# Second layer: down product of the feed-forward and the last layer norm in one stage, by passes over token tiles

## What is computed

```python
    x = layer_norm(DN_ALPHA * x + mix, ln1_w, ln1_b)
    ffn = (jax.nn.silu(x @ ffn_w_gate) * (x @ ffn_w_up)) @ ffn_w_down
    return layer_norm(DN_ALPHA * x + ffn, ln2_w, ln2_b)
```

## Time and profile before

| What | Value |
|---|---|
| Median of 3 runs | 4682.42 us (4680.55 to 4683.03) |
| The profiled execution, own time | 4683.53 us |
| Its span in the profile | 4681.7 us |
| Mean granted TensorE clock | 0.894 of full |
| TensorE, VectorE, ScalarE busy | 80%, 53%, 32% of the span |

### The profile page before, as it was taken

The page is one execution under the profiler, slowest core; times in us unless marked ns, Lnnn a source line. Parts: engine busy times, 40 slices in busy tenths (PEclk is TensorE's granted clock), DMA queues, the critical chain, the costliest instruction groups (busy, mean ns, idle before and its releaser), DMA issues. The chain is left out here.

```text
span 4681.7 us, 62399 instructions
## 1 busy us (share of the span) xinstructions
PE 3759.1 (80%) x25544; PEld 3078.1 (66%) x25544; DVE 2488.5 (53%) x2686; ACT 1494.1 (32%) x1777; POOL 90.8 (2%) x57
## 2 busy tenths in 40 slices
PE   6999948887399999189995545437998788999994
PEld 5888847776377777178883234217996667888783
DVE  5773328944388889354412879664555542111235
ACT  3222114533177777221121232342332221111223
POOL 0000000000100000100000010000000000000002
PEclk8999979998599999589997677669999899999997
DMA  6422226423599999642222131352110432111113
GB/s 244 170 104 87 85 71 204 142 69 143 202 397 399 398 398 358 237 146 103 99 72 80 38 122 65 107 132 72 43 54 9 157 113 63 45 50 45 45 64 144
DMA packets 355375, 652.91 MB, mean 139 GB/s; under 512 B 53896, under 2 KB 149912, under 8 KB 352954
## 3 DMA queue, kind: packets, MB, share of 16 engines
q1 hardware_dynamic: 317482, 524.34, 32.5%
q10 hardware_dynamic: 26864, 83.37, 4.5%
q0 software_dynamic: 10784, 41.70, 2.2%
HBM read 489.23 MB, written 171.65 MB: 141 GB/s over the span
## 5 line engine op out<-in xcount | busy, mean ns | idle before, releaser
L155 PE MATMUL fu_ps<-x3T_hi,fu_w_lo 128*128 128x512 f32 x704 | 275.2, 391 | 9.5 <-DVE fu_w_lo L3055 9.5
L155 PE MATMUL g_ps<-x2T_hi,g_w_lo 128*128 128x512 f32 x704 | 275.1, 391 | 9.1 <-DVE g_w_lo L338 9.1
L156 PE MATMUL fu_ps<-x3T_lo,fu_w_hi 128*128 128x512 f32 x704 | 275.0, 391 | 0.0
L156 PE MATMUL g_ps<-x2T_lo,g_w_hi 128*128 128x512 f32 x704 | 274.8, 390 | 0.0
L157 PE MATMUL g_ps<-x2T_hi,g_w_hi 128*128 128x512 f32 x704 | 274.8, 390 | 0.0
L157 PE MATMUL fu_ps<-x3T_hi,fu_w_hi 128*128 128x512 f32 x704 | 274.8, 390 | 0.0
L382 DVE COPY g_st<-g_ps 128x512 f32<-128x512 f32 x40 | 27.7, 692 | 323.2 <-PE g_ps L157 323.2
L1497 DVE TENSOR_TENSOR moe_wg_lo<-moe_wg,moe_wg_hi 128x2048 fp32r<-128x2048 f32 x68 | 155.6, 2292 | 69.7 <-ACT moe_wg_hi L1451 69.7
L370 DVE SCALAR_TENSOR_TENSOR g_st<-g_pad,g_par,g_st 128x1024 f32<-128x1024 f32 x140 | 179.8, 1285 | 10.8 <-issue 0.4
L155 PE MATMUL g_ps<-h1T_hi,g_w_lo 128*128 128x512 f32 x448 | 175.6, 392 | 7.2 <-DVE g_w_lo L338 7.2
L156 PE MATMUL g_ps<-h1T_lo,g_w_hi 128*128 128x512 f32 x448 | 175.4, 392 | 0.0
(11 more groups left out here) (608 smaller groups left out, 9967.1 us busy)
## 6 DMA issues: line engine op xcount, KB each, us to landing
moe_wg<-in_exp_w_gate SPq DMA_DIRECT2D x68, 1024.0 KB
moe_wu<-in_exp_w_up SPq DMA_DIRECT2D x68, 1024.0 KB
moe_wd<-in_exp_w_down SPq DMA_DIRECT2D x66, 1024.0 KB
g_w<-in_w_in SPq DMA_DIRECT2D x96, 512.0 KB, 4.0
s_conv<-g_st ACTq DMA_DIRECT2D x14, 2048.0 KB, 6.9
s_xs<-g_zero POOLq DMA_DIRECT2D x1, 24064.0 KB
s_ys<-moe_y ACTq DMA_DIRECT2D x47, 512.0 KB, 6.3
moe_x<-s_xs SPq DMA_DIRECT2D x34, 512.0 KB
```

What stands on the lines that cost most here:

```text
L155: pe.matmul(out, l[1], r[0], start=(k == 0), stop=False)
L156: pe.matmul(out, l[0], r[1], start=False, stop=False)
```

## The change

`gemm_deep` for the down product and the `residual_norm` behind it are replaced by one stage, `deep_norm` (tiles also named `fd_`). The product is now made in three passes over token tiles, (0, 1, 2), (3, 4, 5) and (6, 7). A pass runs over k = 0 to 21; a unit n is one k of one pass, 66 units in all. In a unit the tiles of the pass are multiplied by all 1024 output columns, as two matmul columns of 512, into an accumulator of two PSUM banks per tile; four accumulators are used in turn. For each unit 128x1024 weights are loaded (512 KB) and split, and of `hid` only the pass's tokens (384, in the last pass 256 columns) are split. There are three buffers of each; the split halves lie in the memory of `xT`, which is free by then.

The x3 tiles are loaded to `r` (five buffers), at units 3 to 7 and, once the tile before in the buffer is stored, at k = 13 to 15 of the second pass. The norm of a pass's tiles is made in `r` in place while the next pass is multiplied: residual straight from PSUM behind k = 1, sums behind k = 2, centring and squares behind k = 3, variance behind k = 4, roots behind k = 5, the scaling of one tile each behind k = 6, 7 and 8, stores behind k = 10, 11 and 12. The last pass's tiles are normed after the product. The multiplication by the norm weight is on VectorE. `fo` is gone. The parts of `deep_norm` for `router`, `factor` and `sum_out` are not used in this call.

```diff
+def deep_norm(nc, name, aT, w_src, x, w, out, passes, alpha=1.0, bias=None, eps=EPS, factor=None, sum_out=None, room=None,
+              router=None, n_r=NT):
...
+    KT, layer, ND = aT.shape[1], bias is not None, D // P
...
+    NR, NB, NU = 3, 3, NP * KT
+    n_acc = 2 if router else 4
+    with Stage(nc, name) as s:
+        w_raw, r, sq = s.sb("w_raw", [P, NR, D]), s.sb("r", [P, n_r, D]), s.sb("sq", [P, D])
+        wr = s.sb("wr", [P, D])
+        br = s.sb("br", [P, D]) if layer else None
...
+        if room:
+            (w_hi, a_hi), (w_lo, a_lo) = ((h[:, 0:NB], h[:, NB:2 * NB, 0:TP * P]) for h in room)
...
+        acc = s.ps("acc", [P, n_acc, D])
...
+        def unit(n):
+            return n // KT, n % KT
+
+        def side(n):
+
+            g = passes[n // KT]
+            return slice(g[0] * P, g[0] * P + len(g) * P), len(g) * P
...
+            def load(t):
+                if t < NT:
+                    if t >= n_r:
+                        sp.wait_ge(stored[t % n_r], past(16 * (t // n_r)))
+                    sp.dma_start(r[:, t % n_r], x[t * P:t * P + P, :]).then_inc(x_in[t % n_r], 16)
...
+            def store(t):
+                sp.wait_ge(normed, past(t + 1))
+                sp.dma_start(out[t * P:t * P + P, :], r[:, t % n_r]).then_inc(stored[t % n_r], 16)
+
+            for n in range(NU):
+                p, k = unit(n)
+                if n >= NR:
+                    sp.wait_ge(w_low, past(n - NR + 1))
+                sp.dma_start(w_raw[:, n % NR], w_src[k * P:k * P + P, :]).then_inc(w_in[n % NR], 16)
+                if n == 2:
+                    for t, src in ((wr, w),) + (((br, bias),) if layer else ()):
+                        sp.dma_start(t[:, :], src.partition_broadcast(P)).then_inc(c_in, 16)
+                if 3 <= n < 3 + n_r:
+                    load(n - 3)
+                for i, t in enumerate(passes[p - 1] if p else ()):
+                    if k == 5 + i:
+                        store_sum(t)
+                    if k == 10 + i:
+                        store(t)
+                    if k == 13 + i and t + n_r >= n_r:
+                        load(t + n_r)
...
+            for t in passes[-1]:
+                store(t)
+            for b in range(n_r):
+                sp.wait_ge(stored[b], past(16 * len(range(b, NT, n_r))))
...
+            for n in range(NU):
+                p, k = unit(n)
+                pe.wait_ge(w_low, past(n + 1))
+                pe.wait_ge(a_low, past(n + 1))
+                for i, t in enumerate(passes[p]):
+                    if k == 0 and t >= n_acc:
+                        pe.wait_ge(added, past(t - n_acc + 1))
+                    for c in range(2):
+                        mm = products3(pe, acc[:, t % n_acc, c * 512:c * 512 + 512],
+                                       [h[:, n % NB, i * P:i * P + P] for h in (a_hi, a_lo)],
+                                       [h[:, n % NB, c * 512:c * 512 + 512] for h in (w_hi, w_lo)], k, KT)
+                    if k == KT - 1:
+                        mm.then_inc(done, 1)
+                if k < KT - 1:
+                    mm.then_inc(used, 1)
...
+        def free(eng, n):
+
+            if n >= NB:
+                p, k = unit(n - NB)
+                if k == KT - 1:
+                    eng.wait_ge(done, past(passes[p][-1] + 1))
+                else:
+                    eng.wait_ge(used, past(n - NB + 1 - p))
...
+        @block.scalar
+        def _(act):
+            def split(n):
+                p, k = unit(n)
+                o, m = side(n)
+                free(act, n)
+                act.wait_ge(w_in[n % NR], past(16 * (n // NR + 1)))
+                act.activation(w_hi[:, n % NB], w_raw[:, n % NR], ACT.Copy).then_inc(w_high, 1)
+                f = {} if factor is None else dict(scale=fac[:, k:k + 1])
+                act.activation(a_hi[:, n % NB, 0:m], aT[:, k, o], ACT.Copy, **f).then_inc(a_high, 1)
...
+            def total(g):
+                for t in g:
+                    act.wait_ge(added, past(t + 1))
+                    act.activation(sq[:, :], r[:, t % n_r], ACT.Identity, accum_out=mean[:, t:t + 1]).then_inc(sums, 1)
+                    act.wait_ge(sums, past(t + 1))
+
...
+            def square(g):
+                for t in g:
+                    if layer:
+                        act.wait_ge(mean_ok, past(t + 1))
+                        act.activation(sq[:, :], r[:, t % n_r], ACT.Square, bias=nmean[:, t:t + 1],
+                                       accum_out=ssq[:, t:t + 1]).then_inc(squares, 1)
...
+                    act.wait_ge(squares, past(t + 1))
+
+            def take_root(g):
+                for t in g:
+                    act.wait_ge(var_ok, past(t + 1))
+                    act.activation(root[:, t:t + 1], var[:, t:t + 1], ACT.Sqrt).then_inc(root_ok, 1)
...
+            for n in range(NU):
+                p, k = unit(n)
+                split(n)
+                if p:
+                    g = passes[p - 1]
+                    if k == 2 and layer:
+                        total(g)
+                    if k == 3:
+                        square(g)
+                    if k == 5:
+                        take_root(g)
...
+            g = passes[-1]
+            if layer:
+                total(g)
+            square(g)
+            take_root(g)
...
+        @block.vector
+        def _(v):
+            def split(n):
+                p, k = unit(n)
+                o, m = side(n)
+                v.wait_ge(w_high, past(n + 1))
+                v.tensor_tensor(w_lo[:, n % NB], w_raw[:, n % NR], w_hi[:, n % NB], ALU.subtract).then_inc(w_low, 1)
+                v.wait_ge(a_high, past(n + 1))
+                if factor is None:
+                    v.tensor_tensor(a_lo[:, n % NB, 0:m], aT[:, k, o], a_hi[:, n % NB, 0:m], ALU.subtract).then_inc(a_low, 1)
...
+            def residual(g):
+                for t in g:
+                    v.wait_ge(x_in[t % n_r], past(16 * (t // n_r + 1)))
+                    v.wait_ge(done, past(t + 1))
+                    v.scalar_tensor_tensor(r[:, t % n_r], r[:, t % n_r], float(alpha), acc[:, t % n_acc], ALU.mult,
+                                           ALU.add).then_inc(added, 1)
+
+            def centre(g):
+                for t in g:
+                    v.wait_ge(sums, past(t + 1))
+                    v.tensor_scalar(nmean[:, t:t + 1], mean[:, t:t + 1], -1.0 / D, None, ALU.mult).then_inc(mean_ok, 1)
+
+            def variance(g):
+                for t in g:
+                    v.wait_ge(squares, past(t + 1))
+                    v.tensor_scalar(var[:, t:t + 1], ssq[:, t:t + 1], 1.0 / D, float(eps), ALU.mult, ALU.add).then_inc(var_ok, 1)
...
+            def scale(t):
+                o = r[:, t % n_r]
+                v.wait_ge(root_ok, past(t + 1))
+                v.reciprocal(rstd[:, t:t + 1], root[:, t:t + 1])
...
+                v.drain()
+                if layer:
+                    v.tensor_scalar(o, o, nmean[:, t:t + 1], rstd[:, t:t + 1], ALU.add, ALU.mult)
+                    v.drain()
+                    v.tensor_tensor(o, o, wr[:, :], ALU.mult)
+                    v.drain()
+                    v.tensor_tensor(o, o, br[:, :], ALU.add).then_inc(normed, 1)
...
+            for n in range(NU):
+                p, k = unit(n)
+                split(n)
+                if n == 3:
+                    v.wait_ge(c_in, past(32 if layer else 16))
+                if p:
+                    g = passes[p - 1]
+                    if k == 1:
+                        residual(g)
+                    if k == 3 and layer:
+                        centre(g)
+                    if k == 4:
+                        variance(g)
+                    for i, t in enumerate(g):
+                        if k == 6 + i:
+                            scale(t)
...
+            if layer:
+                centre(g)
+            variance(g)
+            for t in g:
+                scale(t)
+            if router:
+                for t in g:
...
@@ -3315,7 +3625,7 @@
     hyena_spectrum(nc, A["c_feats"], A["c_window"], A["hy_filt_w1_2"], A["hy_filt_b1_2"], A["hy_filt_w2_2"],
                    A["hy_filt_b2_2"], A["hy_filt_w3_2"], A["hy_filt_b3_2"], A["hy_filt_w4_2"], A["hy_sin_freq_2"],
                    A["hy_skip_2"], A["c_hft"], spec, top)
-    x3, fo = (scratch(n, [SEQ, D]) for n in ("x3", "fo"))
+    x3 = scratch("x3", [SEQ, D])
     zh, zr = scratch("zh", [HY_W, SEQ]), scratch("zr", [RW_W, SEQ])
     with ExitStack() as own:
         sT = own.enter_context(nc.sbuf_tensor("shT", [P, HY_W // P, SEQ], F32))
@@ -3336,9 +3646,8 @@
         product_norm(nc, "ow", xT, A["w_o_2"], x2, A["ln1_w_2"], A["ln1_b_2"], DN_ALPHA, C["ident"], x3)
         hid = own.enter_context(nc.sbuf_tensor("hid", [P, FFN_H // P, SEQ], F32))
         ffn_up(nc, xT, A["ffn_w_gate_2"], A["ffn_w_up_2"], hid)
-        gemm_deep(nc, "fd", hid, A["ffn_w_down_2"], fo, n_out=2)
```

(4 more changed lines are left out.)

111 lines of the change are left out of this document (added).

## The result

The changed kernel takes 4641.16 us (median of 4 runs, 4635.69 to 4643.20) against 4682.15 of before (4 runs): ratio 0.9911, 95% interval 0.9894 to 0.9928, 41 us faster. The forecast was 4639.6.

What follows compares the result with a forecast made beforehand. TensorE bounds the product; loads, then VectorE, bound the 63.9 us tail. Terms -0.7 - 1.9 + 7.9 - 48.1 = -42.8 us, from 4682.4 to 4639.6 (chance 0.52); range 4631.7 to 4648.

Steps and rivals of the forecast that it cites:

- Start: Start of the down product: smaller splits of 384 and 256 columns bring the first matmul 0.7 us earlier.
- Boundary: Old column boundary of the product: TensorE's waits for the eviction and the split queued behind it go, -1.9 us.
- Weight splits and loads: Product: 66 weight splits and 512 KB loads instead of 22 are covered by TensorE and three buffers, 0 us.
- Norm in pass 2: Norm of pass 1's tiles inside pass 2: splits stay ready before TensorE wants them, 0 us.
- Waits of the last pass: Norm of pass 2's tiles in the last pass: queued norm work makes TensorE wait at k = 4, 7, 8, 9, +7.9 us.
- Tail: Last matmul's end to span's end: only tiles 6 and 7 left to norm, 15.9 us instead of 64.0, -48.1.
- it starts at the low clock either way: Product's first matmul: low clock before and after the change, as it follows a wait of the same kind.
- A: Last pass: the waits are not there, as sums or squares overlap better; -50.7 us, 4631.7; chance 0.12.
- C: Last pass: loads land later, in 7.8 us, sharing the queue with x3 and stores; +9.7 us, 4649.3; chance 0.09.
- D: Product: the ring of three weight buffers becomes the bound, slower than before; +59 us, 4698; chance 0.03.
- B: Last pass: the clock falls in the waits and the last fall is paid, 1.5 to 3 us; 4642; chance 0.22.
- waits of 2.3 lie below both: Last pass: no clock fall taken, as 2.3 us is below earlier waits of 2.75 (low clock after) and 2.62 (high).

Runs made afterwards that it cites:

- passes alone: Changed kernel's three passes and residuals kept, but raw sums stored to DRAM and normed by the old norm stage afterwards; 4666.35 us, ratio 0.9971 to the kernel before.
- scaling left out: Changed kernel with tiles 3 to 5 stored without centring, weight and bias, only their reciprocals kept; 4633.84 us in one profiled execution.
- Spread: Changed kernel with the norm's sums, squares and scaling instructions put one behind each unit of the next pass, stores and reloads later; 4629.64 us.
- sums over one column: Changed kernel with sums and squares of tiles 3 to 5 run over one column instead of 1024; 4631.31 us in one profiled execution.
- the old tail without GpSimd: Kernel before the change, with the last norm's multiplication by the weight on VectorE instead of GpSimd; 4676.62 us, ratio 0.9990.
- two weight buffers: Changed kernel with two raw weight buffers instead of three; 4642.52 us in one profiled execution.
- every load twice: Changed kernel with each unit's weights loaded a second time into spare buffers that nothing reads; 4642.29 us in one profiled execution.

## Why the prediction was right

The forecast of -42.8 us came out as -41.9 in the profile and -41.0 in the medians, and by terms:

- Start, -0.7: -1.0. The split of 384 columns is short (VectorE 0.55 against 1.23 us), and the first load landed 0.3 us sooner.
- Boundary, -1.9: the waits are gone, no pass begins late. Right.
- Weight splits and loads at 0: right, by the passes alone. Landing 3.3 us where I took 3.9.
- Norm in pass 2 at 0: right, TensorE busy for 94.0 of 94.0 us.
- Waits of the last pass (k = 4, 7, 8, 9), 3.2 + 0.1 + 2.3 + 2.3 = 7.9: 3.5 + 0 + 0.6 + 2.2 = 6.3, and 1.6 for the low clock behind k = 4, which was spent before k = 8 wanted its data. The sum is the same, as VectorE sets when k = 9 begins. With the scaling left out, no later wait takes it up, and the 1.6 us are paid. Spread, the waits and the fall both vanish and the product is 8 us shorter.
- Tail, 15.9: 15.8. The squares of tile 7, roots and both scalings are where they were put.
- What failed: the step "it starts at the low clock either way", with the low clock as long as before. Seven spacings from one matmul to the next were long before, 14 after, 0.2 us each: +1.4 us. It is no fixed property of the edit: among the ten profiles with the new start it was 14 in six (the changed kernel twice, scaling left out, sums over one column, passes alone, spread) and 6 to 9 in four, and of the two with the old start it was 7 in one and 12 in the other (the old tail without GpSimd). What sets it is not shown. Less 0.4 us of start and tail it is about the 0.9 us by which the forecast is off.

Of the rivals, A (no waits) and C and D (loads) did not happen. B happened in half: the clock fell, but the fall was not paid, because a later wait for VectorE swallowed it, as the prediction's own sum said it would. The Trainium skill ("TensorE: Matmul & The Clock Gate", HAM oscillation) tells of bursts split by waits, each of which brings the clock down; the wait of 3.3 us agrees, those of 0.44 and 2.02 us behind it do not. My stated reason for expecting no fall at all (waits of 2.3 lie below both rows) was aimed at the wrong wait: the one of 3.3 us lay above both.

Not settled: what scatters the kernels by several us from run to run. The stages before this one differ by that much in profiles of the same code there, and no single one does it: in the twelve profiles the first matmul of the experts starts within 4.4 us, that of the w_o product within 6.9, that of the down product within 8.8.

## What to carry to other kernels

Work that is hidden beside a matrix product must fit unit by unit, not on the sum: VectorE had 44 us of work under 60 of TensorE and still it cost TensorE 8, since three sums, three squares or a whole scaling stood in one piece in an in-order queue with only three units of lead. Put one instruction behind each unit, or put the short pass where nothing is hidden beside it. And cost the queue by hand with start-to-start times from rows of like instructions; it gave the sum of the waits to 0.1 us, and each to 0.3 us but that of k = 8, from which the low clock took the rest.

## Not expected of the hardware

- A wait of 2.0 us of TensorE (sums over one column) was followed by the low clock; one of 2.02 us in the changed kernel was not. Of the waits of 3.3 us, all five profiles with one show the fall. The 2.75 us wait of the earlier trace rows is thus no lower end.
- The low clock behind such a wait lasted some 8 matmuls at 0.43 us in the changed kernel, and some 14 with two weight buffers and with every load twice.
- The new weight loads landed in 3.3 us (median) while 157 GB/s were moving, sooner than the first of the old ones on idle queues (3.9) and than the first of the new ones (3.6). The new ones take whole rows of 1024 columns, the old ones half rows; whether that is why was not tried.
